# Summing head norms, key norm and bonus on column tiles and spreading them back from row tiles, in a three-branch decoder step

## The reference, cut to what matters

```
def _head_norm(x, gain, bias, eps):              # once per branch and layer, 3 times in a layer
    xc = xf - jnp.mean(xf, axis=-1, keepdims=True)
    y = xc * lax.rsqrt(jnp.mean(xc * xc, axis=-1, keepdims=True) + eps)
    ...
# RWKV-7 branch: key norm and bonus
kk = kk / jnp.maximum(jnp.sqrt(jnp.sum(kk * kk, axis=-1, keepdims=True)), 1e-12)
bonus = jnp.sum(hd(r * kr * p['rw_rk']), axis=-1, keepdims=True) * hd(vr)
# the gated sum of the branches
gates = jax.nn.sigmoid(zgate.reshape(B, T, N_BRANCH, D_MODEL))
out = jnp.sum(gates * proj, axis=2) @ p['w_out']
```

## Time and profile before

| | |
|---|---|
| median of 3 runs | 1620.1 us (1619.22 to 1621.28) |
| the profiled execution | 1617.53 us, of which the span is 1615.7 us |
| PE busy | 1569.1 us, 97% of the span, 17365 matmul records |
| DVE busy | 564.0 us, 35% |
| ACT busy | 293.8 us, 18% |
| POOL busy | 50.5 us, 3% |
| mean granted TensorE clock | 0.992 |

### The profile page before, as it was taken

One profiled execution on the slowest core, in us unless ns is written; L12 is line 12 of the kernel. 1 busy time (PEld: TensorE's weight loads), 2 busy tenths in 40 slices (PEclk: granted clock), 3 DMA queues, 4 the chain that ended last, 5 costly groups with the idle time before them and its releaser, 6 DMA issues.

```text
span 1615.7 us, 38502 instructions
## 1 busy us (share of the span) xinstructions
PE 1569.1 (97%) x17365; PEld 1254.2 (78%) x17365; DVE 564.0 (35%) x1276; ACT 293.8 (18%) x642; POOL 50.5 (3%) x62
## 2 busy tenths in 40 slices
PE   8999999999999999999999999999989999899887
PEld 6878777887777777777887777877778797798665
DVE  5133476746110000014236278644152231122113
ACT  1432113323110000012332123122120000000001
POOL 1000010110000000000000000200000000000000
PEclk9999999999999999999999999999999999999998
DMA  8224345213533343355224353126769888899880
GB/s 328 105 105 148 127 134 139 80 42 68 190 131 130 108 166 130 115 188 182 86 79 177 135 131 118 41 61 200 302 249 362 334 289 282 319 330 369 318 318 32
DMA packets 59027, 288.48 MB, mean 179 GB/s; under 512 B 21560, under 2 KB 22008, under 8 KB 32376
## 3 DMA queue, kind: packets, MB, share of 16 engines
q1 hardware_dynamic: 48056, 268.08, 46.3%
q0 software_dynamic: 2272, 15.73, 2.7%
q10 hardware_dynamic: 8544, 2.33, 1.0%
HBM read 275.22 MB, written 10.89 MB: 177 GB/s over the span
## 4 chain that ended last, share of the span: by engine, by line
PE 95%; DVE 2%; issue 2%; DMA 1%; ACT 0%; SPq 0%; DVEq 0%
PE ps L1372 15%; PE ps L825 15%; PE ps L1257 11%; PE ps L1484 11%; PE ps L1449 7%; PE ps L1264 6%; PE ps L1493 5%; PE ps L1319 4%; PE ps L817 3%; PE ps L1113 2%; PE ps L1397 2%; DMA ring<-in_mix 1%; PE ps L835 1%; PE ps L840 1%; PE ps L1089 1%
## 5 line engine op out<-in xcount | busy, mean ns | idle before, releaser
L825 PE MATMUL ps<-xn,ring 128*128 128x288 f32 x928 | 236.6, 412 | 0.0
L825 PEld LDWEIGHTS ps<-xn,ring 128*128 128x128 f32 x928 | 176.1, 193 | 49.2 <-issue 1.9
L1257 PE MATMUL ps<-xn,ring 128*128 128x288 f32 x768 | 199.1, 409 | 0.3 <-DMA ring<-in_mix 0.2
L1257 PEld LDWEIGHTS ps<-xn,ring 128*128 128x128 f32 x768 | 143.5, 190 | 43.1 <-issue 4.6
L1484 PE MATMUL ps<-xn,ring 128*128 128x288 f32 x704 | 171.1, 406 | 0.7 <-DVE xn L1920 0.7
L1484 PEld LDWEIGHTS ps<-xn,ring 128*128 128x128 f32 x704 | 133.7, 190 | 37.7 <-issue 0.8
L1372 PE MATMUL ps<-y_ml,arena 128*64 128x96 f32 (+5 forms) x3584 | 141.0, 241 | 10.9 <-issue 10.4
L1372 PEld LDWEIGHTS ps<-y_ml,arena 128*64 128x64 f32 x3584 | 138.0, 139 | 15.9 <-issue 15.8
L1449 PE MATMUL ps<-arena,mixed 128*32 128x256 f32 x2024 | 112.1, 379 | 2.2 <-issue 2.2
L1449 PEld LDWEIGHTS ps<-arena,mixed 128*32 128x32 f32 x2024 | 65.2, 110 | 46.1 <-issue 3.4
L1493 PE MATMUL ps<-arena,ring 128*128 128x288 f32 x352 | 85.7, 406 | 0.0
(11 more groups left out here) (459 smaller groups left out, 1682.5 us busy)
## 6 DMA issues: line engine op xcount, KB each, us to landing
arena<-in_egu SPq DMA_DIRECT2D x56, 1024.0 KB, 7.2
ring<-in_mix SPq DMA_DIRECT2D x46, 1024.0 KB, 5.0
arena<-in_edown SPq DMA_DIRECT2D x40, 1024.0 KB, 6.3
ring<-in_mix SPq DMA_DIRECT2D x48, 768.0 KB, 4.3
ring<-in_egu SPq DMA_DIRECT2D x32, 1024.0 KB, 7.4
ring<-in_gu SPq DMA_DIRECT2D x22, 1024.0 KB, 4.9
ring<-in_down SPq DMA_DIRECT2D x16, 704.0 KB, 4.0
arena<-in_C POOLq DMA_DIRECT2D x2, 2048.0 KB, 8.0
```

The lines of the kernel that those rows point to most:

```text
L825: last = mm(bank[:, 0:T], ring[:, s, w0:w0 + P], (xn if n else xgain)[:, k, :], start=(k == 0), stop=(k == KT - 1))
L1257: last = mm(ps[:, bank, 0:T], ring[:, s, P * k:P * k + P], xn[:, k, :], start=(k == 0), stop=(k == KT - 1))
```

## The change

The four sums over squares become four products with 32-column weights (`C("ones", TS)`, or the new `C("sum64", TS)`), each placed on its own 32 columns of the array and so on its own 32 partitions of one bank, 4. Root and reciprocal then run over one 128 x 288 tile instead of four. Four products with 32-row weights (`C("lead", P)`, or the new `C("lead64", P)`), each on its own 32 rows of the array, spread the result back over banks 4 to 7, and `finish` reads it from PSUM. PE now has two waits in a head norm instead of one run, and fills stand between sums and spread. The same is done for key norm and bonus, where the fills go from 24 and 24 to 12, 4 and 18; the 14 products that this frees go to later places, 12 of them into the last head norm. Two unit sums, which ran behind `w_pre`, now run after the first of the four `blocks`. The memset of `KRm` (1.87 us at line 2271) is split over two chunks. `closing` takes its four gate banks in the order 0, 2, 3, 1, so that only the fourth waits for the last unit's sum. In `rwkv_chunks` ACT takes the fourth chunk's sigmoid behind its output copy.

```diff
-PLACES = [("norm", 24), ("shift", 40), ("lora", 8), ("square", 24), ("bonus", 24), ("pre", 16), ("gram", 6), ("first", 22),
-          ("tokens", 6), ("chunk0", 6)] + [(f"chunk{c}", 5) for c in range(1, NC - 2)] + [(f"chunk{NC - 2}", 4), ("samples", 2)]
+PLACES = [("norm", 24), ("shift", 40), ("lora", 8), ("square", 12), ("bonus", 4), ("later", 18), ("pre", 16), ("gram", 6),
+          ("first", 22), ("tokens", 5), ("chunk0", 7)] + [(f"chunk{c}", 5) for c in range(1, NC - 2)] + \
+         [(f"chunk{NC - 2}", 4), ("samples", 4), ("centre", 4), ("spread", 8)]
...
+            def head_sums(q, sq, ones):
+
+                pe.wait_ge(hn_x.sem, 4 * q + 4)
+                pe.wait_ge(hn_s.sem, 4 * q + 4)
                 for j in range(4):
-                    pe.wait_ge(hn_s.sem, 4 * q + j + 1)
-                    pe.wait_ge(hn_x.sem, 4 * q + j + 1)
-                    mm(ps[:, 4 + j, 0:T], ones, sq[:, j, :], start=True, stop=True).then_inc(hn_v.sem, 1)
+                    last = mm(ps[rows_of(j), 4, 0:T], ones, sq[:, j, :], start=True, stop=True)
+                last.then_inc(hn_tensor.sem, 1)
+
+            def head_spread(q, sq, lead):
+
+                pe.wait_ge(hn_r.sem, q + 1)
+                for j in range(4):
+                    last = mm(ps[:, 4 + j, 0:T], lead[rows_of(j)], sq[rows_of(j), 0, :], start=True, stop=True)
+                last.then_inc(hn_tensor.sem, 1)
...
                 for j in range(4):
-                    mm(ps[:, 4 + j, 0:T], C("ones64", P), rw_e1[:, j, :], start=True, stop=True)\
-                        .then_inc(w_ss.sem, 1)
-                fill(l, 24)
+                    last = mm(ps[rows_of(j), 4, 0:T], C("sum64", TS), rw_e1[:, j, :], start=True, stop=True)
+                last.then_inc(w_ss.sem, 1)
+                fill(l, 12)
+                pe.wait_ge(*w_kr(l))
+                for j in range(4):
+                    last = mm(ps[:, 4 + j, 0:T], C("lead64", P)[rows_of(j)], rw_e1[rows_of(j), 0, :], start=True, stop=True)
+                last.then_inc(w_ss.sem, 1)
                 pe.wait_ge(*w_rk(l))
...
+                    last = mm(ps[rows_of(j), 2, 0:T], C("sum64", TS), rw_e2[:, j, :], start=True, stop=True)
+                last.then_inc(w_bo.sem, 1)
+                fill(l, 4)
+                pe.wait_ge(*w_boe(l))
+                pe.wait_ge(*w_kd(l))
+                for j in range(4):
+                    last = mm(ps[:, 4 + j, 0:T], C("lead64", P)[rows_of(j)], rw_e2[rows_of(j), 0, :], start=True, stop=True)
+                last.then_inc(w_bo.sem, 1)
+                fill(l, 18)
+                pe.wait_ge(*w_bd(l))
...
                 pe.wait_ge(*ml_sca(l, 2))
-                head_norm(3 * l, ml_o, ml_sq, C("cent128", P), C("ones", P))
-                groups(l, AT_MLNORM, AT_ROTATE)
-                pe.wait_ge(*hn_q(l, 4))
+                centred(3 * l, ml_o, C("cent128", P))
+                groups(l, AT_MLNORM, AT_MLNORM + 1)
+                head_sums(3 * l, ml_sq, C("ones", TS))
+                groups(l, AT_MLNORM + 1, AT_MLNORM + 2)
+                head_spread(3 * l, ml_sq, C("lead", P))
+                groups(l, AT_MLNORM + 2, AT_ROTATE)
+                pe.wait_ge(*hn_used(l))
...
-                fill(l, 64)
+                centred(3 * l + 1, ret_o, C("cent128", P))
+                fill(l, 6)
+                head_sums(3 * l + 1, ret_sq, C("ones", TS))
+                fill(l, 8)
+                head_spread(3 * l + 1, ret_sq, C("lead", P))
+                fill(l, 50)
...
+                centred(3 * l + 2, rw_o, C("cent64", P))
+                fill(l, 4)
+                head_sums(3 * l + 2, rw_sq, C("sum64", TS))
+                fill(l, 8)
+                head_spread(3 * l + 2, rw_sq, C("lead64", P))
                 closing(l)
...
+                dve.wait_ge(*w_ssq(l))
+                link(TSC(rw_e1[:, 0, :], rw_e1[:, 0, :], 1e-12, None, MAX))
+                dve.reciprocal(rw_e1[:, 0, :], rw_e1[:, 0, :]).then_inc(w_kr.sem, 1)
                 for j in range(4):
                     last = STT(rw_e2[:, j, :], zs[:, j, :], V(l, "rk", j), rw_kp[:, j, :], MUL, MUL)
                 last.then_inc(w_rk.sem, 1)
-                unit_sums(l, "square", 0, 1)
-                dve.wait_ge(*w_ssq(l, 4))
-                link(TSC(rw_e1, rw_e1, 1e-12, None, MAX))
-                last = dve.reciprocal(rw_e1, rw_e1)
-                unit_sums(l, "square", 1)
-                link(last)
-                link(TT(rw_kk, rw_kk, rw_e1, MUL))
+                unit_sums(l, "square")
+                dve.wait_ge(*w_ss(l, 2))
+                for j in range(4):
+                    last = TT(rw_kk[:, j, :], rw_kk[:, j, :], ps[:, 4 + j, 0:T], MUL)
+                last.then_inc(w_kd.sem, 1)
+                unit_sums(l, "bonus")
...
                 link(last)
+                unit_sums(l, "later")
                 TT(rw_e2, rw_e1, rw_lw, SUB).then_inc(w_F.sem, 1)
...
                 link(TT(rw_a, rw_a, rw_kk, MUL))
-                unit_sums(l, "bonus", 1)
                 dve.wait_ge(*w_E(l))
...
                 blocks(KR, 0, rw_kk, rw_e2)
+                unit_sums(l, "pre")
                 blocks(KR, 1, zs[:, 0:4, :], rw_e1)
...
                 dve.sem_inc(w_pre.sem, 1)
-                unit_sums(l, "pre")
```

More of the change, by code:

```diff
@@ L582, in build, with hn_sum, hn_spread @@
         ml_out, co_ok, so_ok = sig("ml_out"), sig("conv_out_ok"), sig("shift_out_ok")
[L583 to L584 removed]
+        hn_c, hn_s, hn_x, hn_y = sig("hn_c", 12), sig("hn_s", 12), sig("hn_x", 12), sig("hn_y", 3)
+        hn_tensor, hn_q, hn_r, hn_used = sig("hn_tensor", 6), sig("hn_root", 3), sig("hn_reciprocal", 3), sig("hn_used")
+        def hn_sum(q):
+            return hn_tensor.sem, 2 * q + 1
+        def hn_spread(q):
+            return hn_tensor.sem, 2 * q + 2
         r_tensor, r_vector, r_scalar = sig("retention_tensor", 12), sig("retention_vector", 8), sig("retention_scalar", 7)
@@ L589, in build @@
         r_oe, r_ose, r_ote, r_spe = (Part(r_scalar, k) for k in (0, 4, 5, 6))
[L590 to L593, removed]
+        w_tensor, w_scalar, w_vector = sig("rwkv_tensor", 34), sig("rwkv_scalar", 21), sig("rwkv_vector", 24)
+        w_lora, w_ss, w_bo, w_vt, w_g1, w_g2 = (Part(w_tensor, k) for k in (0, 12, 14, 16, 21, 31))
+        w_thl, w_lorae, w_ssq, w_boe, w_E, w_vte = (Part(w_scalar, k) for k in (0, 1, 13, 14, 15, 16))
+        w_zs, w_sq, w_kr, w_rk, w_kd, w_bd, w_F, w_pre, w_g1e, w_g2e, w_x0, w_km, w_umv = (Part(w_vector, k) for k in
+                                                                          (0, 1, 2, 3, 4, 5, 6, 7, 8, 18, 21, 22, 23))
         w_zuv, rw_y, w_ob = sig("w_zero", 4), sig("rw_y"), sig("w_ob", 6)
@@ L1142, in rwkv_tokens @@
                     last.then_inc(w_bt.sem, 1)
-                fill(l, 4)
+                fill(l, 3)
             def head_cols(h):
@@ L1206, in rwkv_chunks @@
                 rwkv_rest(l, 0)
-                fill(l, 1)
+                fill(l, 2)
                 for c in range(NC - 1):
@@ L1635, in head_norm @@
                     A(sq[:, j, :], src[:, j, :], ACT.Square).then_inc(hn_s.sem, 1)
-                for j in range(4):
-                    act.wait_ge(hn_v.sem, 4 * q + j + 1)
-                    A(sq[:, j, :], ps[:, 4 + j, 0:T], ACT.Sqrt, scale=1.0 / n, bias=C("eps", 1, P, eps))\
-                        .then_inc(hn_q.sem, 1)
+                act.wait_ge(*hn_sum(q))
+                A(sq[:, 0, :], ps[:, 4, 0:T], ACT.Sqrt, scale=1.0 / n, bias=C("eps", 1, P, eps)).then_inc(hn_q.sem, 1)
                 if q % 3 == 1:
@@ L1642, in head_norm @@
                     unit_gates(q // 3, "shift")
+                if q % 3 == 2:
+                    unit_gates(q // 3, "spread")
             def mlstm_gates(l):
@@ L1715, in rwkv_prepare @@
                 unit_gates(l, "lora")
-                for j in range(4):
-                    act.wait_ge(*w_ss(l, j + 1))
-                    A(rw_e1[:, j, :], ps[:, 4 + j, 0:T], ACT.Sqrt).then_inc(w_ssq.sem, 1)
+                act.wait_ge(*w_ss(l, 1))
+                A(rw_e1[:, 0, :], ps[:, 4, 0:T], ACT.Sqrt).then_inc(w_ssq.sem, 1)
                 unit_gates(l, "square")
+                act.wait_ge(*w_bo(l, 1))
+                A(rw_e2[:, 0, :], ps[:, 2, 0:T], ACT.Copy).then_inc(w_boe.sem, 1)
                 unit_gates(l, "bonus")
+                unit_gates(l, "later")
                 act.wait_ge(*w_F(l))
@@ L1785, in closing @@
                         act.wait_ge(u_add.sem, i * 4 + (base + k - 3))
-                        A(gates[:, k, :], ps[:, k, 0:T], ACT.Sigmoid).then_inc(u_sig.sem, 1)
+                        A(gates[:, k, :], ps[:, GATE_BANK[k], 0:T], ACT.Sigmoid).then_inc(u_sig.sem, 1)
                 turns.pass_over(len(UNITS) + len(OUTS))
@@ L1926, in head_norm @@
                     dve.tensor_copy(src[:, j, :], ps[:, 4 + j, 0:T]).then_inc(hn_x.sem, 1)
-                for j in range(4):
-                    dve.wait_ge(hn_q.sem, 4 * q + j + 1)
```

(20 more changed lines are left out.)

52 lines of the change are left out of this document (26 added, 26 removed).

## The result

Over ten runs of each kernel on one chip, the changed kernel takes 1627.88 us (median; 1619.49 to 1630.85) and the kernel before 1619.51 (1615.67 to 1621.28). The ratio is 1.0048, with a 95% interval of 1.0035 to 1.0061: slower, by 8 us. The profiled run of the changed kernel took 1628.12 us with a span of 1626.3, 10.6 above the span before. So the forecast (slower; 1629.7, range 1622.5 to 1634.5) holds. What matters is whether it holds for the reasons that it gave.

What follows compares the result with a forecast made beforehand. PE's own order was taken as the bound, its chain covering 95% of the span. Tile sets less `w_rk` waits -2.6, gaps +10.0 and clock +2.2 make +9.6 us: median 1629.7, range 1622.5 to 1634.5.

Steps and rivals of the forecast that it cites:

- The two sums in front of `w_pre`: Before `rwkv_gram`: unit 9's sum waits for PE's 120th product, so PE stands 5.27 us; 10.0 us added in two layers.
- The tile sets: Head norms, key norm and bonus: four tiles run as one product, shape changes cost 0.1 to 0.2; 0.28 off per norm.
- Rival A: Sets at streaming speed, weight loads hidden at shape changes: 9.8 us off at ten places, total about 1622.5; chance 0.08.
- The wait for `w_rk`: Key norm and bonus: bonus operands stand behind DVE's reciprocal, so PE waits about 0.27 us per layer.
- The clock: Behind each new gap: half-rate clock adds 1.05 to 1.1 us, 2.2 in all; bounds 0 and 2.6 each.
- "No wait that I find" for the small edits: Gate-bank order, halved memset, later sigmoid: zero PE wait while covered; a missed cover would cost 0.5 to 1 us each.
- The sum: Whole run: -2.6 + 10.0 + 2.2 = +9.6 us, giving a median of 1629.7.

Runs made afterwards that it cites:

- the version with identity products: Changed kernel plus ten identity products with unread results in front of PE's wait for `w_pre`: 1624.31 us, ratio 1.0035 to the kernel before.
- doubling: Changed kernel with every set of four column-tile or row-tile products issued twice, same result: 1640.67 us in one run.
- the version with unit 8's sum earlier: Changed kernel with unit 9's sum behind `w_pre` and unit 8's in front of DVE's wait for the exponentials: 1613.7 us, ratio 0.9971 to before.
- the control: The changed kernel run again without edit, beside the follow-up versions: 1627.74 us, ratio 1.0067 to the kernel before.
- the version without a gap: Changed kernel, unit 9's sum behind `w_pre`, unit 8's before the exponentials' wait, two fill products moved ahead of `rwkv_gram`: 1610.04 us, again 1611.49 on another chip.
- the other direction's version: Kernel before with only its `pre` unit sum moved from behind `w_pre` to behind the first `blocks`: 1633.8 us, ratio 1.0103.

## Why the prediction was right, point by point

**The two sums in front of `w_pre`: right, in mechanism and size.** Predicted: 10.0 us in two layers, by a gap of 5.27 in place of 0.25. The profile calls 5.10 of it idle, from the modelled end of PE's last product. Taken from start to start, as the prediction did, PE is ready at 286.04, where the version with identity products starts the first of them, and the gap is 5.26: 5.01 more than before in each layer, 10.0 in all. The parts fit as well: DVE was expected to stand 2.6 us for the 120th product and stood 2.44, the chain behind that product was 0.27 + 0.87 + 5.10 and took 291.30 - 285.07 = 6.23. The gram was expected at 292.16 and came at 291.30, mostly because PE came to the key norm at 256.40 and not at the 257.03 from which the prediction placed it; the gap didn't change by that, as the prediction said of it ("whatever PE's place"). Unit 9's sum put behind the handover takes it away and the loss with it, and the same move in the old kernel makes it.

**The tile sets: right in kind, their gain a little too large.** Predicted from neighbouring shapes: 0.60 for sums, 0.69 for spreads, 0.19 for each return, so 1.67 for a head norm's sums and spread in place of 1.95. The head norm of retention after, layer 0:

```profile
214.20 3.07 PE L1292 MATMUL ps<-xn,ring 128*128 128x288 f32 x12
217.20 0.69 PE L857 MATMUL ps<-arena,con 128*32 128x288 f32 x8
...
222.60 3.18 PE L1292 MATMUL ps<-xn,ring 128*128 128x288 f32 x12
```

A set of sums takes 0.62 (256.40 to 257.02) and a spread 0.70 (266.56 to 267.26). Around them each series of fills is longer than 0.485 a product: six products take 3.00 instead of 2.91 in front of the sums, and 3.02 behind the spread, from 222.60 to 225.62. So a change of shape costs 0.09 in front of a set and 0.11 behind it, together 0.20 where 0.19 was predicted. That makes 1.72 for the norm, 0.23 off instead of 0.28. The two head norms in front of the key norm brought 0.36 us net, predicted 0.56: in both layers PE gains 0.36 on before from the mLSTM's sums to the key norm. That the key norm starts 0.63 earlier in layer 0 is no measure of it, as two other differences lie in front of it (the point on the sum). Rival A, sets at streaming speed, fell: doubling shows that streaming is the cost of the second set alone.
The Trainium skill, TensorEngine Tiling (Array Packing), Key Properties, says that a change of tiling mode drains TensorE, and Theoretical Speedup gives up to four times for 32-wide tiles. Both hold here at once: a second set at the full rate of 0.48, and 0.14 or 0.22 us more for the first, with 0.09 and 0.11 around it. For a single set between plain products the second rule eats most of what the first gives.

**The wait for `w_rk`: size off.** 0.27 us a layer were predicted. The spread ahead of it took 0.76 to the next start where a spread without a wait takes 0.70, which leaves 0.06.

**The clock: right, size too small.** Predicted: 1.1 us behind each gap, from the experts' end. Measured: 3.47 instead of 1.99, 1.5 us, at a granted clock of 0.57; inside the bounds of 0 and 2.6. The ten identity products show that it is the idle that does it. The neighbour that I took had gaps of 0.72 and 1.62 us, not 5.
The Trainium skill, TensorE: Matmul & The Clock Gate, Part 1, has the throttled state as the default and activity as what releases it; the 0.57 with the gap and the 1.00 with dummies in it agree.

**"No wait that I find" for the small edits: right of the changed kernel, but for a reason that it didn't give.** In the three head norms PE has no new wait. But the prediction left the bank order and the halved memset at zero as if they were free; undone, they cost 0.77 and 0.57 us a layer. Its clause "a missed cover would cost 0.5 to 1 us each" had that size. Zero was the price of the edit, not the worth of it.

**The sum: right, and nearer than its terms by luck.** Predicted -2.6 + 10.0 + 2.2 = 9.6. PE is 8.7 us later at routing in the profiled runs, and two parts of that aren't the change's. One lies at the very start: the first long series in front of the first norm takes 4.83 us to the next start after (10.05 to 14.88) and 3.59 before (9.88 to 13.47), and with it PE is 1.4 later before any changed work has run.
The other is the mLSTM's sums, where before's profiled run spent more time at the lower clock (last section): from their first product to the next stage 9.58 us before and 7.90 after in layer 0, 11.22 and 9.58 in layer 1, 3.3 in all to before's disadvantage. Without both the layers are 10.6 later. The gaps are 10.0 of it and the clock behind them 3.0, which leaves -2.4 for the tile sets and all else, against -2.6 predicted with 0.5 of waits for `w_rk` in it. So the measured sum is -2.4 + 10.0 + 3.0 = 10.6.
The last 1.9 of the span's 10.6 come in routing and experts. Stalls for issue are not it: over all of PE's lines they are 20.5 us before (14.9, 3.4 and 2.2) and 21.2 after (20.4 and 0.8), and 22.7 in the version with unit 8's sum earlier, which is faster than before. But the granted clock was 0.94 after and 0.97 before over the 53 us from 1177 to 1230, about 1.6 us of work by that, and nothing of the change runs there. So the profiled spans differ by 10.6 because 1.4 and 1.9 on the one side and 3.3 on the other cancel. On the medians the change cost 8.4 and 9.6 us.

**What stays open.** Of the ten first runs of the changed kernel, seven took 1627.6 to 1630.9 and three 1619.5 to 1622.9. The three had mean granted clocks of 0.991 to 0.993, the seven 0.984 to 0.990. So the clock goes with it; why it did better in three runs of one program isn't known, and no run of the control was as fast. The same holds for the version without a gap: PE's timeline gives it 1.0 us in layer 0 by the end of the closing (428.4 against 429.4), though it was 0.5 behind at the first norm, and some 2.6 in both layers by such differences (0.5 of that are the two old waits of 0.25), and the runs give it 8.1 and 8.3. Its mean clock was 0.993 on both chips against 0.991 of before. A mean clock that is 0.002 higher does 0.2% more in the same time, about 3 us of 1615, so the two together make some 6 of the 8. That is an estimate from these means. Which part of the clock's rise the shorter waits bring, the runs don't tell.

## What to carry to other kernels

In an engine's queue, work that waits for a late product must not stand ahead of a handover that the same engine's partner waits for: here one unit's sum of 0.87 us cost 3.4 of the 5.1 us of gap and 1.5 of clock in each layer, and moving it behind the handover gave both back. Before adding work ahead of a handover, count the place of the product it needs among the products that PE issues before its own wait; if it is one of the last, the whole chain behind it shows as idle, however fast everything else is. Small tiles are worth their rate only in series: a lone set between full-size products pays for two changes of shape, and here a head norm got 0.2 of the 1.0 us that the rate promises.

## What the hardware did that I had not expected

Column tiles and row tiles differ in the cost of the change: 0.14 and 0.22 us within the first set. In front of either the series is 0.09 us longer, and behind either 0.11. A gap of 1.72 us in mid-layer left the clock up, at 1.00 over the six microseconds that hold it and what follows (version with unit 9's sum late), while one of 5.10 brought it to 0.57, and so did the one of 4.13 in the other direction's version (0.57 from 298 to 302):

```profile
284.00:290.00 6.00, 4.28 (x42) 3.42 (x41) 5.55 (x18) 0.12 (x1) 0.00 (x0) 1.00 0.41 131
```

The clock also fell where PE had not stood. Stage and timeline rows of before, then of after, behind the smallest products of the mLSTM's sums in layer 0 (4 x 1 to 4 x 32 elements), with fill products following:

```profile
91.00:96.00 5.00, 5.00 (x32) 4.05 (x30) 1.69 (x8) 2.08 (x4) 0.00 (x0) 0.78 0.37 152
```
```profile
94.61 5.33 PE L825 MATMUL ps<-xn,ring 128*128 128x288 f32 x16
```
```profile
91.00:96.00 5.00, 5.00 (x63) 4.00 (x62) 0.99 (x6) 1.69 (x2) 0.00 (x0) 1.00 0.64 267
```
```profile
95.63 4.05 PE L836 MATMUL ps<-xn,ring 128*128 128x288 f32 x16
```

PE is busy for all of the 5 us in both, and yet the same 16 records take 5.33 in the one and 4.05 in the other. From the first of the small products to the next stage the same operations take 9.58 us (90.20 to 99.78) and 7.90 (91.61 to 99.51), at 0.78 and 1.00 over the rows shown. It isn't a thing of one run: in the twelve profiled runs here the granted clock falls behind these products in layer 1 every time, and in layer 0 in eight. So a place where PE does very little per instruction is, like a gap, one where the clock may fall, in one run and not in the next. It cost 1.7 us in layer 0 here, and 3.3 before and 1.7 after in layer 1 (11.22 and 9.58, against the same 7.90). That the small products are the reason is argued from the place alone; no run changed them.

And the mean granted clock of whole runs was lowest in the kernels with a gap of over 4 us: 0.987 in the control and in the version made from before, 0.988 in the first ten runs of the changed kernel. The others, with gaps of 0 to 1.7 us, had 0.990 to 0.993, without an order by the gap among them. The stretches at half rate that make up this mean lie mostly outside the layers' gaps, so a gap in one stage may cost a little in others. That is a pattern over eight kernels, before among them, on several chips, not a shown cause.
